# Second weight matrix of each expert with two neighbouring rows per partition, in a mixture-of-experts step on one core

## The reference

```
h = RMSNorm(x) * (1 + scale1) + shift1          # scales and shifts from the conditioning vector
z = h @ w_in                                    # seven parts of 1024 columns
y_a = (a_b * conv3(a_c * a_in)) @ w_out_a
y_b = silu(LN(conv31(b_val * sigmoid(b_gate)))) @ w_out_b
x = x + gate1 * RMSNorm((sigmoid(g_a) * y_a + sigmoid(g_b) * y_b) @ w_o)
h = RMSNorm(x) * (1 + scale2) + shift2
scores = sigmoid(h @ w_router)                  # 64 experts, 8 groups, top 8 of the best 4 groups
act[e] = silu(h @ w1[e]) * (h @ w3[e]) * gate   # w1, w3: 64 x 1024 x 256
routed = sum over the 8 chosen e of act[e] @ w2[e]   # w2: 64 x 256 x 1024
x = x + gate2 * RMSNorm(routed + shared expert)
```

## Time and profile before

| | |
|---|---|
| median of 3 runs | 1365.47 us (1364.73 to 1366.45) |
| the profiled execution | 1364.27 us, its span 1362.5 us |
| TensorE busy over the span | 1272.5 us (93%) |
| bytes moved by DMA | 336.71 MB, of which 295.00 MB on q1 |
| mean granted clock of TensorE | 0.971 of full speed |

### The profile page before, as it was taken

The page is one execution under the profiler, slowest core; times in us unless marked ns, Lnnn a source line. Parts: engine busy times, 40 slices in busy tenths (PEclk is TensorE's granted clock), DMA queues, the critical chain, the costliest instruction groups (busy, mean ns, idle before and its releaser), DMA issues.

```text
span 1362.5 us, 26053 instructions
## 1 busy us (share of the span) xinstructions
PE 1272.5 (93%) x9305; PEld 945.0 (69%) x9306; DVE 497.9 (37%) x816; ACT 347.3 (25%) x596; POOL 361.1 (27%) x369
## 2 busy tenths in 40 slices
PE   6799999999998998969899999999999999999995
PEld 4599999999998998958555555555555555555532
DVE  1466668666673565068221100000000000000067
ACT  4332322323232512343111111111111112111221
POOL 1144445444463243300121221121122112212200
PEclk8699999999998999989899999999999999999988
DMA  9844353442412232237999899999999989974086
GB/s 312 263 143 140 103 190 92 144 149 82 148 34 60 76 93 77 78 115 289 379 346 360 329 420 372 410 417 418 417 417 398 395 351 418 399 293 162 31 301 262
DMA packets 155878, 336.71 MB, mean 247 GB/s; under 512 B 12733, under 2 KB 97213, under 8 KB 137366
## 3 DMA queue, kind: packets, MB, share of 16 engines
q1 hardware_dynamic: 137888, 295.00, 57.8%
q0 software_dynamic: 14544, 34.10, 6.7%
q10 hardware_dynamic: 3406, 7.05, 1.5%
HBM read 322.18 MB, written 33.78 MB: 261 GB/s over the span
## 4 chain that ended last, share of the span: by engine, by line
PE 79%; DVE 6%; issue 6%; DMA 5%; ACT 2%; POOL 1%; SPq 1%; ACTq 0%; DVEq 0%; POOLq 0%
PE ps L1512 26%; PE ps L1527 13%; PE ps L1334 10%; PE ps L1335 10%; PE ps L1336 10%; PE ps L1505 4%; PE ps L1275 2%; DMA ring<-in_w_ada_dram 1%; PE ps L1519 1%; PE ps L1287 1%; SPq L281 1%; DVE ring L1238 1%; DMA out_dram<-ring 1%; POOL wsplit L459 1%; DMA ring<-in_w_in_dram 1%
## 5 line engine op out<-in xcount | busy, mean ns | idle before, releaser
L1512 PE MATMUL ps<-w,xe 128*64 (+1 forms) x3200 | 356.6, 381 | 12.3 <-issue 12.3
L1512 PEld LDWEIGHTS ps<-w,xe 128*64 128x64 f32 x3200 | 236.6, 137 | 148.0 <-issue 47.4
L1334 PE MATMUL ps<-h_s_hi,wsplit 128*128 128x260 f32 x1024 | 292.2, 285 | 2.9 <-DVE h_lo_m_hi L932 2.7
L1336 PE MATMUL ps<-h_s_hi,wsplit 128*128 128x260 f32 x1024 | 289.7, 283 | 0.0
L459 POOL TENSOR_TENSOR wsplit<-ring,wsplit 128x1024 fp32r<-128x1024 f32 x80 | 192.3, 2404 | 320.9 <-ACT wsplit L623 320.9
L1335 PE MATMUL ps<-h_lo_m_hi,wsplit 128*128 128x260 f32 x896 | 253.8, 283 | 0.0
L1217 DVE TENSOR_TENSOR rs<-sg,ps 128x256 f32<-128x256 f32 x50 | 21.1, 421 | 505.4 <-PE ps L1512 505.4
L1334 PEld LDWEIGHTS ps<-h_s_hi,wsplit 128*128 128x128 f32 x1024 | 193.6, 189 | 11.2 <-issue 6.7
L1336 PEld LDWEIGHTS ps<-h_s_hi,wsplit 128*128 128x128 f32 x1024 | 193.8, 189 | 0.0
L1527 PE MATMUL ps<-w,eactT 128*64 (+1 forms) x800 | 182.7, 598 | 10.9 <-ACT eactT L861 10.9
L1335 PEld LDWEIGHTS ps<-h_lo_m_hi,wsplit 128*128 128x128 f32 x896 | 169.8, 190 | 0.0
(11 more groups left out here) (283 smaller groups left out, 1367.8 us busy)
## 6 DMA issues: line engine op xcount, KB each, us to landing
w<-in_w_dram SPq DMA_DIRECT2D x192, 1024.0 KB, 14.4
ring<-in_w_in_dram SPq DMA_DIRECT2D x56, 512.0 KB, 3.9
ring<-in_w_ada_dram SPq DMA_DIRECT2D x12, 2048.0 KB, 9.3
ring<-y_rows SPq DMA_DIRECT2D x8, 1024.0 KB, 9.9
act<-y_rows SPq DMA_DIRECT2D x8, 1024.0 KB, 14.2
ring<-in_w_out_a_dram SPq DMA_DIRECT2D x8, 512.0 KB, 3.7
ring<-in_w_out_b_dram SPq DMA_DIRECT2D x8, 512.0 KB, 3.7
ring<-in_w_o_dram SPq DMA_DIRECT2D x8, 512.0 KB, 3.6
```

What stands on the lines that cost most here:

```text
L1334: mm(ps[:, bank + h, 0:HT], wsplit[:, b, 0, k, :], hi[:, k, p:q], start=(k == 0), stop=False)
L1336: ins = mm(ps[:, bank + h, 0:HT], wsplit[:, b, 1, k, :], hi[:, k, p:q], start=False, stop=(k == C - 1))
L1512: ins = mm(ps[a * STRIP:(a + 1) * STRIP, bank, 0:FE], xe[:, k, a * STRIP:(a + 1) * STRIP], w[a][:, k, :], start=(k == 0), stop=(k == C - 1))
```

## The change

The load of w2 is laid out so that partition p gets the neighbouring rows 2p and 2p + 1 of w2[e], one run of 8 KB. So that the contraction still pairs each value of `eact` with its row, the two transposes of `act_T` no longer take columns 0 to 127 and 128 to 255 of `eact` but its even and its odd columns, with a stride of two elements (8 bytes). Number, order and size of all instructions stay as they are, and so do the waits.

```diff
@@ down_weights(e, slot)
                 sp.dma_start(w2raw[slot],
-                             w2[0, ds(e, 1), :, :].rearrange("a (k p) n -> p (a k) n", p=P)).then_inc(w2_in[slot], 16)
+                             w2[0, ds(e, 1), :, :].rearrange("a (p k) n -> p (a k) n", p=P)).then_inc(w2_in[slot], 16)
@@ act_T(src, bank)
+                v = src.rearrange("s (m f) -> s f m", f=FT)
                 for f in range(FT):
-                    ins = tr(ps[:, bank, f * P:(f + 1) * P], src[:, f * P:(f + 1) * P], ident[:, :])
+                    ins = tr(ps[:, bank, f * P:(f + 1) * P], v[:, f, :], ident[:, :])
                 return ins
```

## The result

Timed beside each other in ten runs each, the kernel before takes 1366.14 us (median, 1363.63 to 1367.53) and the changed one 1369.57 us (1368.27 to 1371.60). The ratio is 1.003 with a 95% interval of 1.002 to 1.004: 3.4 us slower. The time lies in the predicted range of 1364.5 to 1371.5. It doesn't lie at the forecast of +1.9 us, and it is outside the forecast's own range, which ended at 1369.0; it is nearer to the rival of the slow strided loads, which gave +4.4.

What follows compares the result with a forecast made beforehand. TensorE was taken to bound the expert stage, with weights early. Terms 0 + 0 + 1.3 + 0.6 + 0 = +1.9 us on the median 1365.47 gave 1367.4 us; 8-in-10 range 1364.5 to 1371.5, forecast's own 1365.8 to 1369.0.

Steps and rivals of the forecast that it cites:

- the rival of the slow strided loads: Transposes of act_T: stride 2 as slow as stride 8, +4.4 us in all, 1369.9 us; chance 0.30.
- The rival in which the loads bound a part: Expert stage: issue time before L1512 hides waits for weights, so 3.1 us come off, 1362.4 us; chance 0.06.
- The load, term 0: Loads of w2: 8192 fewer packets save 3.1 us of DMA time, hidden because the loads are early by 18 us or more.
- The strided transposes, term 0: Two transposes of act_T in each of 50 steps: stride 2 taken to cost nothing, being nearer to 1 than 8.
- the upper one with one load exposed: Transposes of act_T: one load per step delayed as at stride 8, 50 x 0.05 = 2.5 us.
- The prediction's own sign of being wrong: Transposes of act_T: the prediction is wrong if L1519's pair takes longer than 0.44 us.
- its two terms of the head: Before the expert steps: the first gather lands later, +1.3 us, and the tiles of h land later, +0.6 us.
- The first gather, +1.3: Gather before the first step: its 9 rounds alternate with larger w2 packets, so it and TensorE's first step come 1.3 us later.
- the case that the prediction named with a negative sign: TensorE's first step: the clock rises at the same moment as before, winning back about half the gather's delay, -0.65 us.
- Its other case, as much again at the low clock: TensorE's first step: as much again follows at the low clock, losing another 1.7 us.
- The tiles of h, +0.6: Tiles on q10 beside experts 0 to 2's loads: L809 released 1.3 us later, less 0.68 us of cover, +0.6 us.
- The gathers in the stage, term 0: Gathers before L1505: 9 rounds add 0.6 us, hidden by a cover of 1.6 us, so 0.

Runs made afterwards that it cites:

- the load alone: The kernel before with only the new load of w2 and the transposes of before: ratio 1.0002 (0.9993 to 1.0011) against the kernel before.
- the wait: One more wait on SyncE, issuing the loads of experts 3 to 5 only after the first gather landed; added to the kernel before: ratio 0.9986.
- the added block: Kernel before plus, behind TensorE's last matmul, groups of 16 transposes or plain matmuls at several strides; one execution, transpose loads 140 ns at stride 1, otherwise 193 to 239.

## Why the prediction was right and where it was wrong

**What bounds the kernel** was read rightly. The DMA engines look full, yet the load alone moved nothing: weights that land a median of 1.5 us earlier (14.2 us after issue, 15.7 before) are worth nothing to a TensorE that never waits for them. The rival in which the loads bound a part (-3.1 us) is excluded by that run, whose interval ends at -1.0.

**The load, term 0:** right, with the number of packets as forecast.

**The strided transposes, term 0:** this is the step that failed, although the time fell in the range. The prediction took the price of stride 2 to be that of stride 1, to which it is nearer than to 8, and so put the term at nothing. It measured 205 ns a load against 140, and 3.2 us in the stage. Mechanism and exposure were right: on the chain in every step, one load of two exposed, 50 times in full. The choice between the ends was wrong, and the upper one with one load exposed, 2.5 us, was itself too low, because stride 2 is dearer than stride 8. The prediction's own sign of being wrong, a pair longer than 0.44 us, came true: 0.51. With 3.2 in place of 0 its sum would have been +5.1, and with the head as measured (0.7 in place of 1.9) +3.9. That the forecast was off by 1.5 us and not by 3.2 is luck: its two terms of the head were too large by 1.2 together, with the opposite sign. And the range held the result only because the slow stride had been kept as its upper end.

The rule of the Trainium skill that was weighed there (SBUF — State Buffer, Door 1: The DMA port swizzle: two hits on a line of 16 bytes suffice) doesn't hold for the loads of transposes: 209 ns at two hits a line, 193 at one with stride 8. The measurement decides. For the loads of plain matmuls the four rows agree with it: 196 ns with two hits, 329 with one.

**The first gather, +1.3:** right in kind, a little large. It takes 9.35 to 9.55 us in the five profiled kernels with the new load and without the wait, and 8.46 to 8.62 in the five with the old load, so 0.9 us more, not 1.3. In the changed kernel the first up matmuls gave 0.3 back: the clock rose 2.7 us after their start in place of 3.4, which is the case that the prediction named with a negative sign. Its other case, as much again at the low clock, was seen too, in four executions, and costs 1.6 us; the changed kernel's profiled execution was spared it.

**The tiles of h, +0.6:** wrong, it was 0. From the first issue of weights ScalarE's copy L809 was released after 30.49 us before and after 30.63 in the changed kernel, where 1.3 us more were forecast. Its next copy did come 1.1 us later, but TensorE doesn't wait for that one. In the timeline of the changed kernel, the copy released by the DMA, and the index matmuls:

```profile
633.39 1.02 ACT L809 ACTIVATE act<-ps 128x1024 f32<-128x1024 f32 x1 [3.29 <-DMA h_rows<-act]
...
649.46 0.64 PE L1490 MATMUL ps<-act 128*128 128x132 f16 x8 [0.63 <-DVE act L1138]
```

TensorE still has 0.63 us to spare at L1490, as against 0.68. Part of the reason stands in the packets of q10, in the 2 us from 20 us after the first issue of weights, before (621.13 to 623.13) and after (622.76 to 624.76):

```profile
q10 hardware_dynamic: 20, 0.07, 9.0%
```

```profile
q10 hardware_dynamic: 70, 0.22, 27.3%
```

In the 10.2 us ahead of these the tiles of x had fallen back by 51 packets (372 in place of 423), about 3 rounds, and the pause that q10 had before took in all of it: the prediction had counted on 1.4 us there, and it was enough. In the next 8 us q10 moved 307 packets in place of 333; why the first tile still landed only 0.14 us later stays open.

**The gathers in the stage, term 0:** right. The stage with the load alone is 619.2 us, to the tenth that of before.

**The chances.** The strided rival had 0.30 and the forecast 0.44. "Slower" at 0.41 came true, by a little over the bound of 0.2%, at which the interval begins.

## What to carry to other kernels

A layout that helps a DMA pays only if somebody waits for that DMA; read who waits before counting packets. A permutation that a layout forces on the computation has a price that depends on the place: here it was nothing in two PSUM reads off TensorE, 3 us in a weight load of a transpose, 9 in a jumping write of VectorE and 17 in TensorE's moving operand, and it is best put into an access whose length it doesn't change. A price between two measured strides can't be interpolated: a block of a few dozen operations at the kernel's end measures it.

## What the runs showed of the hardware that was not expected

- In the added block a transpose of float32 loads a contiguous operand of 128 columns in 140 ns, and one with any of the six strides tried in 193 to 239 ns; strides 2 and 4 take 209, 6 takes 239, 8 takes 193. Plain matmuls take 192, 196, 329 and 335 ns at strides 1, 2, 4 and 8. The cause of the order among the strides isn't known.
- Between the landing of the first gather and the first up matmul lie 4.3 us both before (658.78 to 663.09) and with the load alone (658.44 to 662.73), although the eight transposes between them take 1.41 us in one and 1.96 in the other. Something other than they sets that time; the profile calls it issue.
- Two executions of kernels that are the same up to the first up matmuls differed by 1.6 us in these (8.46 and 10.07 us), as the clock rose 2.8 or 5.9 us after their start.
- A VectorE product of 128 x 256 float32 takes 421 ns, with a PSUM operand read at stride 2 as well, and 609 ns when its write jumps 128 elements at every second one.
